# The matrix engine multiplies the former item's values ahead of this item's turns

## The chip, the cores and the metric

One core of one Trainium2 chip runs the whole program. The metric is the device time of one execution in microseconds, median of several runs. The kernel is written in direct instructions for five engines, each with a queue of its own that runs in order: the matrix engine (TensorE, PE), VectorE (DVE), ScalarE (ACT), GpSimd (POOL) and the DMA queues. They wait for one another by semaphores.

## What is computed

512 tokens of width 1024 pass through two layers of a first block (latent attention, "MLA", with 8 heads over all 512 keys, beside a dilated attention with three groups of 8 heads, both gated) and one layer of a second block (a feed-forward part, a linear recurrence beside a windowed attention with 16 heads, a second feed-forward part). All products are made from high and low halves in three matmuls. The parts that the change touches are the three kinds of attention:

```python
# MLA: every query tile of 128 against 512 keys
s = (q_nope @ k_nope + q_rope @ k_rope) * scale
o = softmax(s) @ v
# dilated: three groups, (window, dilation) = (128,1), (512,4), (2048,16)
o_g, lse_g = banded_attention(q_g, k_g, v_g)
out = sum_g softmax(lse)[g] * o_g
# second block: window of 128 keys and a chunk, a bias by distance, a sink logit for each head
p = softmax(concat([q @ k * HEAD_DIM ** -0.5 + bias, sink]))[..., :-1]
o = p @ v
```

## The kernel before

The matrix engine bounds most of the program with long rows of 128x512 matmuls (`feature_major`, `token_major`, the helper `three` in lines 962 to 965). Between them lie seven attentions: `("dil", L, hh)` for two layers and two halves of the heads (8 items each), `("mla", L)` for two layers (16 items each), and `("swa",)` in the second block (16 items). An item is one tile of 128 queries for two heads (four in the second block's, as two pairs), and items run in groups of four tiles, t = 0 to 3. In the second block's attention the item with t = 0 has only half of the keys and is narrower in every step.

For each item n:

- `scores(n)` (PE, line 1085) writes the logits of both halves b = 0, 1 into a pair of PSUM banks; the pairs alternate.
- `maxima(n)` (DVE, line 2049, in MLA line 2060) adds the mask and takes the row maxima.
- `exp_of_item(n)` (ACT, lines 1558, 1562, 1565 and 1572) exponentiates both halves into PR.
- `turn(n)` (PE, line 1097) transposes PR block by block into bank 4 (b = 0) and bank 5 (b = 1). It waits for the exponentials of each half, and for the copy of item n-1 out of the same bank.
- `turned(n)` copies bank 4 (DVE, line 2078) and bank 5 (ACT, line 1583) into PT, which has two buffers.
- `values(n)` (PE, line 1126) waits for both copies and multiplies PT by the values into banks 6 and 7; the last item of a group releases `result`.
- In MLA, at the end of each group, DVE inverts the row sums and spreads them over a tile (`sums_spread`, lines 2086 and 2089), PE transposes them (`spread_sums`, line 1109), and the result is multiplied by them.

DVE and ACT go through the items in the same manner: in round n they first do `maxima(n + 1)` or `exp_of_item(n + 1)` and then `turned(n)`. The first two `scores` of an attention go ahead of the loop, followed by a filler (another product); the loop begins with `turn(n0)`. After the loop come the values of the last item, in MLA with the row sums ahead of them. GpSimd splits two chunks of weights during each attention (`split_in`, lines 892 and 895).

The order of the work is written out by hand: each engine's program is one function, and nothing reorders it.

Of the kernel before, what the change touches and what calls it, by code (L numbers as in the profile page):

```python
# [82 lines left out]
class Plan:  # L83
# [33 lines left out]
    def filler(self, key, by):  # L117

        self.event(key)
        self.pair[key] = 3  # L120
        self.by[key] = by
        out = self.act_out if by == "a" else self.dve_out
        out[key] = len(out) + 1
        self.add_chunk(key, KD, CW, key)
# [220 lines left out]
def build_program(nc, a, out):  # L345
# [3 lines left out]
    with ctx:  # L349
# [155 lines left out]
        def bank(i, n=1):  # L505
            return PS[:, i * S:(i + n) * S]
# [189 lines left out]
        def score_products(it):  # L696

            t, j = it["t"], it["j"]
            tok = slice(t * P, (t + 1) * P)
            got = []  # L700
            if it["kind"] == "mla":
                for i, (q, k) in enumerate(((QNH, KNH), (QNH, KNL), (QNL, KNH))):
                    for b in range(2):
                        got.append((b, 0, S, q[rows_of(b), j, tok], k[rows_of(b), j, :], i == 0))
                for q, k in ((QRH, KRH), (QRH, KRL), (QRL, KRH)):
                    for b in range(2):
                        rows = slice((2 * j + b) % 4 * ROPE, (2 * j + b) % 4 * ROPE + ROPE)
                        got.append((b, 0, S, q[rows, j // 2, tok], k[rows, :], False))
            elif it["kind"] == "dil":
                jj = it["jj"]  # L710
                for block in range(NT):
                    for b in range(2):
                        g = max(block - 1, 0)
                        q, k = (QK[rows_of(b), 2 * g + x, jj, :] for x in range(2))
                        k = near_keys(k, (t - 1 + block) % NT) if block < 2 else k[:, tok]
                        got.append((b, block * P, P, q[:, tok], k, block == 0))
            else:
                n = min(t + 1, 2) * P
                for u in range(2):
                    for b in range(2):  # L720
                        got.append((b, u * 2 * P, n, QS[rows_of(b), 2 * j + u, tok],
                                    K2[rows_of(b), j, (t + 1) * P - n:(t + 1) * P], u == 0))
            return got
# [30 lines left out]
        def blocks_of(it):  # L754
            return (0, 2) if it["kind"] == "swa" and it["t"] == 0 else range(NT)
# [194 lines left out]
        def _(pe):  # L950
            def take_pair(key):

                prev = pl.reuse.get(key)
                if prev is not None:
                    if "x" in pl.by[prev]:
                        pe.wait_ge(f_copied, KD)
                    if "a" in pl.by[prev]:
                        pe.wait_ge(act_out, pl.act_out[prev])
                    if "d" in pl.by[prev]:
                        pe.wait_ge(dve_out, pl.dve_out[prev])  # L960
# [107 lines left out]
            def results_taken(n):  # L1068
                by_dve, by_act = results_before(n)
                if by_dve:  # L1070
                    pe.wait_ge(o_dve, by_dve)
                if by_act:
                    pe.wait_ge(o_act, by_act)

            def attention(name, filler):
                n0, n1 = pl.item_at[name]
                kind = name[0]

                def scores(n):
                    it = pl.items[n]  # L1080
                    take_pair(("item", n))
                    last = [None, None]
                    for b, c0, w, q, k, start in score_products(it):
                        acc = bank(2 * pl.pair["item", n] + b)
                        last[b] = nc.tensor.matmul(acc[:, c0:c0 + w], q, k, start=start, stop=True,  # L1085
                                                   skip_group_check=True)
                    for b in range(2):
                        last[b].then_inc(acc_ready, 1)

                def turn(n):  # L1090
                    it = pl.items[n]
                    for b in range(2):
                        pe.wait_ge(p_ready, 2 * n + 1 + b)
                        if n > 0:
                            pe.wait_ge(pt_act if b else pt_dve, n)
                        for k in blocks_of(it):
                            last = nc.tensor.transpose(bank(4 + b)[:, k * P:(k + 1) * P],  # L1097
                                                       PR[:, n % 2, b * S + k * P:b * S + (k + 1) * P], IDN[:, :])
                        last.then_inc(t_ready, 1)

                def spread_sums(n):

                    it = pl.items[n]
                    g = 4 * it["L"] + it["j"]
                    pe.wait_ge(rl_ready, g + 1)
                    if g:
                        pe.wait_ge(gated_a, g)
                    for t in range(NT):
                        last = nc.tensor.transpose(bank(7)[:, t * P:(t + 1) * P],
                                                   RLB[:, 2 * t:2 * t + 2, :].rearrange("p h d -> p (h d)"), IDN[:, :])  # L1110
                    last.then_inc(rlt_ready, 1)

                def values(n):
                    it = pl.items[n]
                    pe.wait_ge(pt_dve, n + 1)
                    pe.wait_ge(pt_act, n + 1)
                    if it["first"]:
                        results_taken(n)
                    if n == n0:
                        if kind == "swa":  # L1120
                            pe.wait_ge(dve_out, pl.dve_out[filler_of[name]])
                        elif kind == "dil":
                            pe.wait_ge(act_out, pl.act_out[filler_of[name]])
                            pe.wait_ge(v0_in, 16 * 12 * (2 * it["L"] + it["hh"] + 1))
                    for dst, k, v, start, stop in value_products(it):
                        last = nc.tensor.matmul(dst, v, PT[:, n % 2, k * P:(k + 1) * P], start=start, stop=stop,  # L1126
                                                skip_group_check=True)
                    last.then_inc(pv_done, 1)

                scores(n0)  # L1130
                scores(n0 + 1)
                results_taken(n0)
                filler()
                if kind == "mla":
                    pe.wait_ge(act_out, pl.act_out["uv", name[1], 1])
                for n in range(n0, n1):
                    if n0 + 1 < n + 1 < n1:
                        scores(n + 1)
                    turn(n)
                    if n > n0:  # L1140
                        if kind == "mla" and pl.items[n - 1]["last"]:
                            spread_sums(n - 1)
                        values(n - 1)
                if kind == "mla":
                    spread_sums(n1 - 1)
                values(n1 - 1)
# [170 lines left out]
            for L in range(DEPTH):  # L1317
                for hh in range(2):
                    for i, (w, g) in enumerate(DILATED_ORDER):
                        if L == 0 and hh == 0 and i < 2:  # L1320
                            continue
                        if w == "v":
                            if hh == 0 and g == 0:
                                if L == 0:
                                    pe.wait_ge(small_dve, 3)
                                    pe.wait_ge(act_out, pl.act_out["xt", 3])
                                else:
                                    results_taken(pl.item_at["mla", L - 1][1])
                            token_major((w, L, hh, g))
                        else:  # L1330
                            feature_major((w, L, hh, g), new=("x", L) if hh == 0 and i == 0 else None,
                                          norm=("x", L) if hh == 0 and i == 1 else None)
                    pe.wait_ge(rope_done, pl.rope["k", L, hh, 2])
                    attention(("dil", L, hh), lambda: token_major(("v", L, hh, 2)))
# [91 lines left out]
            for j in range(8):  # L1426
                feature_major(("gate", j))
                if j < 4:
# [6 lines left out]
                    for m in range(2):  # L1435
                        for t in range(NT):
                            n = 2 * (NT * m + t)
# [1248 lines left out]
```

## Time and profile before

| | us |
|---|---|
| median of 3 runs | 2161.89 (2161.06 to 2163.26) |
| the profiled execution | 2162.84 |
| its span, first to last instruction | 2161.0 |
| PE busy in it | 2124.9 (98%) |
| DVE, ACT, POOL busy | 1136.9, 765.7, 123.6 |
| PE stalls in front of the turns (line 1097) | 7.5 |
| mean granted clock of PE | 0.997 of 2.4 GHz |

Busy times are of one execution. Starts are in us from the start of the span. A group "x8 1.09" of small matmuls lasts from the first start to the modelled end of the last; the next group on the engine can start before that end, so durations of steps are best taken from start to start.

### The profile page before, as it was taken

How to read it: one execution, taken by the hardware profiler on the slowest of the kernel's cores; microseconds unless marked ns; L12 is line 12 of the kernel's file. 1: busy time of each engine (PE TensorE's matmuls, PEld its weight loads, DVE VectorE, ACT ScalarE, POOL GpSimd, SP SyncE). 2: the span in 40 equal slices, each digit the busy share in tenths (PEclk: the TensorE clock that was granted, in tenths of full speed). 3: DMA queues.
4: the chain of work that ended last, by engine and by line, in shares of the span. 5: the costliest groups of instructions: out<-in, count | busy, mean ns of one | idle time of the engine just before them, and what ended most of it. 6: DMA issues, size and time to landing. Idle time of an engine off the chain costs nothing.

```text
span 2161.0 us, 28431 instructions
## 1 busy us (share of the span) xinstructions
PE 2124.9 (98%) x11767; PEld 1754.6 (81%) x11767; DVE 1136.9 (53%) x1535; ACT 765.7 (35%) x1224; POOL 123.6 (6%) x110
## 2 busy tenths in 40 slices
PE   8999999999999999999999999999999999999998
PEld 6888988678888887788888887787788887888887
DVE  5655557645655557654444445775653446333333
ACT  4251424532242425543222224353643234222222
POOL 0111100200011100200000003000000002000000
PEclk9999999999999999999999999999999999999999
DMA  6313222113313122113333224234022332332321
GB/s 186 99 59 116 80 59 81 40 40 109 100 47 118 60 70 70 40 59 97 97 97 97 98 98 127 79 117 136 21 78 98 98 98 88 96 98 91 100 95 65
DMA packets 158097, 189.04 MB, mean 87 GB/s; under 512 B 4194, under 2 KB 147876, under 8 KB 157860
## 3 DMA queue, kind: packets, MB, share of 16 engines
q1 hardware_dynamic: 153204, 174.41, 25.6%
q0 software_dynamic: 4608, 13.00, 1.9%
q8 instruction: 81, 1.33, 0.3%
q14 instruction: 28, 0.23, 0.0%
q10 hardware_dynamic: 176, 0.07, 0.0%
HBM read 182.20 MB, written 7.36 MB: 88 GB/s over the span
## 4 chain that ended last, share of the span: by engine, by line
PE 91%; DVE 5%; ACT 2%; POOL 1%; issue 1%; DMA 0%; POOLq 0%; DVEq 0%; ACTq 0%
PE PS L963 25%; PE PS L965 25%; PE PS L964 25%; PE PS L1085 5%; PE PS L1126 3%; PE PS L1097 3%; POOL X L930 1%; PE PS L971 1%; PE PS L975 1%; PE PS L972 1%; PE PS L1239 1%; PE PS L1044 0%; DVE WL L1941 0%; DVE UL L1994 0%; DVE TMP L2279 0%
## 5 line engine op out<-in xcount | busy, mean ns | idle before, releaser
L963 PE MATMUL PS<-UH,WH 128*128 128x512 f32 x1632 | 642.7, 394 | 7.5 <-DVE WL L2351 4.7
L965 PE MATMUL PS<-UH,WL 128*128 128x512 f32 x1632 | 637.0, 390 | 0.0
L964 PE MATMUL PS<-UL,WH 128*128 128x512 f32 x1632 | 636.4, 390 | 0.0
L1482 ACT ACTIVATE WH<-WS 128x2048 fp32r<-128x2048 f32 x98 | 187.9, 1918 | 618.1 <-PE PS L965 602.5
L963 PEld LDWEIGHTS PS<-UH,WH 128*128 128x128 f32 x1632 | 307.2, 188 | 75.4 <-DVE UL L1994 6.0
L965 PEld LDWEIGHTS PS<-UH,WL 128*128 128x128 f32 x1632 | 306.9, 188 | 64.7
L964 PEld LDWEIGHTS PS<-UL,WH 128*128 128x128 f32 x1632 | 307.3, 188 | 62.9 <-issue 0.7
L1941 DVE TENSOR_TENSOR WL<-WS,WH 128x2048 fp32r<-128x2048 f32 x98 | 224.4, 2290 | 229.9 <-ACT WH L1482 229.8
L2211 DVE TENSOR_TENSOR WL<-WS,WH 128x2048 fp32r<-128x2048 f32 x44 | 100.7, 2288 | 151.2 <-ACT WH L1636 151.2
L1636 ACT ACTIVATE WH<-WS 128x2048 fp32r<-128x2048 f32 x44 | 84.4, 1917 | 248.9 <-PE PS L965 246.7
L963 PE MATMUL PS<-WH,UH 128*128 128x256 f32 x416 | 118.6, 285 | 0.9 <-DVE PT L2310 0.9
L964 PE MATMUL PS<-WL,UH 128*128 128x256 f32 x416 | 117.7, 283 | 0.0
L965 PE MATMUL PS<-WH,UL 128*128 128x256 f32 x416 | 117.7, 283 | 0.0
L1097 PE MATMUL PS<-IDN,PR 128*128 128x128 f32 x624 | 88.5, 280 | 7.5 <-ACT PT L1583 2.5
L1097 PEld LDWEIGHTS PS<-IDN,PR 128*128 128x128 f32 x624 | 66.7, 140 | 30.8 <-issue 18.2
L1126 PE MATMUL PS<-PT,ARENA 128*64 128x128 f32 x1248 | 84.7, 279 | 0.0
L963 PEld LDWEIGHTS PS<-WH,UH 128*128 128x128 f32 x416 | 79.7, 192 | 2.3 <-issue 1.6
L964 PEld LDWEIGHTS PS<-WL,UH 128*128 128x128 f32 x416 | 79.8, 192 | 0.5 <-issue 0.2
L965 PEld LDWEIGHTS PS<-WH,UL 128*128 128x128 f32 x416 | 79.8, 192 | 0.0
L1126 PEld LDWEIGHTS PS<-PT,ARENA 128*64 128x64 f32 x1248 | 66.6, 136 | 12.6 <-issue 12.6
L2078 DVE COPY PT<-PS 128x512 f32<-128x512 f32 (+1 forms) x80 | 53.8, 672 | 36.1 <-PE PS L1097 36.1
L963 PE MATMUL PS<-HH,WH 128*128 128x512 f32 x176 | 68.5, 389 | 0.0
(312 smaller groups left out, 3090.9 us busy)
## 6 DMA issues: line engine op xcount, KB each, us to landing
WS<-in_ffn_w SPq DMA_DIRECT2D x66, 1024.0 KB, 5.2
WS<-in_w_in SPq DMA_DIRECT2D x61, 1024.0 KB, 5.3
WS<-in_w_out SPq DMA_DIRECT2D x8, 1024.0 KB, 5.1
WS<-in_w_gate SPq DMA_DIRECT2D x8, 1024.0 KB, 5.5
WS<-in_w_attn_out SPq DMA_DIRECT2D x4, 1024.0 KB, 5.1
WS<-in_w_lru_out SPq DMA_DIRECT2D x4, 1024.0 KB, 5.2
WS<-in_w_o SPq DMA_DIRECT2D x4, 1024.0 KB, 5.1
bias_skewed<-bias_rows POOLq DMA_DIRECT2D x1, 3072.0 KB, 13.4
```

Source lines behind the costliest of these rows:

```text
L930: nc.gpsimd.tensor_tensor(X[:, k, :], old[:, k, :], SUMMED[k][:, :], ALU.add).then_inc(x_new, 1)
L963: nc.tensor.matmul(dst, sh, mh, start=start, stop=False, skip_group_check=True)
L964: nc.tensor.matmul(dst, sh, ml, start=False, stop=False, skip_group_check=True)
L965: return nc.tensor.matmul(dst, sl, mh, start=False, stop=stop, skip_group_check=True)
L1085: last[b] = nc.tensor.matmul(acc[:, c0:c0 + w], q, k, start=start, stop=True, skip_group_check=True)
L1097: last = nc.tensor.transpose(bank(4 + b)[:, k * P:(k + 1) * P], PR[:, n % 2, b * S + k * P:b * S + (k + 1) * P], IDN[:, :])
L1126: last = nc.tensor.matmul(dst, v, PT[:, n % 2, k * P:(k + 1) * P], start=start, stop=stop, skip_group_check=True)
L1482: nc.scalar.activation(WH[:, c % 2, 0:kt * n], staged(c, kt * n), ACT.Copy).then_inc(w_hi, 1)
L1636: nc.scalar.activation(WH[:, c % 2, :], WS[:, c % 2, :], ACT.Copy).then_inc(w_hi, 1)
L1941: tt(WL[:, c % 2, 0:kt * n], staged(c, kt * n), WH[:, c % 2, 0:kt * n].bitcast(F32), ALU.subtract).then_inc(w_split, 1)
L2078: nc.vector.tensor_copy(used_half(it, PT[:, n % 2, 0:S]), used_half(it, bank(4))).then_inc(pt_dve, 1)
L2211: tt(WL[:, c % 2, :], WS[:, c % 2, :], WH[:, c % 2, :].bitcast(F32), ALU.subtract).then_inc(w_split, 1)
```

## The change

In the loop of `attention` in the matrix engine's program, `values(n - 1)`, and in MLA at group ends `spread_sums(n - 1)` with it, go ahead of `turn(n)`. Before, round n issued scores(n+1), turn(n), values(n-1); after, it issues scores(n+1), values(n-1), turn(n). All seven attentions use this loop. The programs of the other engines, all waits and all buffers stay as they are.

```diff
                 for n in range(n0, n1):
                     if n0 + 1 < n + 1 < n1:
                         scores(n + 1)
-                    turn(n)
                     if n > n0:
                         if kind == "mla" and pl.items[n - 1]["last"]:
                             spread_sums(n - 1)
                         values(n - 1)
+                    turn(n)
                 if kind == "mla":
                     spread_sums(n1 - 1)
                 values(n1 - 1)
```

## Rows read from the trace of the kernel before

**Rows 1.** The page, busy us by engine, share of the span and instructions.

```profile
PE 2124.9 (98%) x11767; PEld 1754.6 (81%) x11767; DVE 1136.9 (53%) x1535; ACT 765.7 (35%) x1224; POOL 123.6 (6%) x110
```

**Rows 2.** Groups by line: busy us, mean ns, idle before and its releasers.

```profile
L1097 PE MATMUL PS<-IDN,PR 128*128 128x128 f32 x624 | 88.5, 280 | 7.5 <-ACT PT L1583 2.5 <-ACT ARENA L1790 2.2 <-DVE PT L2078 1.8
```

**Rows 3.** Windows, first to last attention: busy of PE, PEld, DVE, ACT, POOL; PEclk; DMA.

```profile
125.40:1557.40 1432.00, 1416.66 (x8429) 1164.97 (x8427) 817.02 (x1230) 540.80 (x978) 99.94 (x76) 1.00 0.26 82
```

**Rows 4.** Timeline, first dilated attention, steady state: start, us, engine, line, operation.

```profile
129.54 1.16 PE L1085 MATMUL PS<-ARENA 64*128 64x128 f32 x16
130.63 1.09 PE L1097 MATMUL PS<-IDN,PR 128*128 128x128 f32 x8
131.66 1.09 PE L1126 MATMUL PS<-PT,ARENA 128*64 128x128 f32 x16
132.68 1.16 PE L1085 MATMUL PS<-ARENA 64*128 64x128 f32 x16
133.45 0.61 ACT L1583 ACTIVATE PT<-PS 128x512 f32<-128x512 f32 x1
133.77 1.09 PE L1097 MATMUL PS<-IDN,PR 128*128 128x128 f32 x8
```

**Rows 5.** Timeline, tail of the same attention (its last item is number 7).

```profile
142.10 1.16 PE L1085 MATMUL PS<-ARENA 64*128 64x128 f32 x16
...
145.62 0.63 PE L1097 MATMUL PS<-IDN,PR 128*128 128x128 f32 x4 [0.31 <-DVE PT L2078]
146.01 0.61 ACT L1583 ACTIVATE PT<-PS 128x512 f32<-128x512 f32 x1
146.76 0.63 PE L1097 MATMUL PS<-IDN,PR 128*128 128x128 f32 x4 [0.51 <-ACT PT L1583]
147.32 1.97 PE L1126 MATMUL PS<-PT,ARENA 128*64 128x128 f32 x32
147.43 0.60 ACT L1583 ACTIVATE PT<-PS 128x512 f32<-128x512 f32 x1 [0.81 <-PE PS L1097]
```

**Rows 6.** Timeline, head of the same attention: scores(2) and ScalarE's copy of item 0.

```profile
126.40 1.16 PE L1085 MATMUL PS<-ARENA 64*128 64x128 f32 x16
127.08 0.62 ACT L1583 ACTIVATE PT<-PS 128x512 f32<-128x512 f32 x1
```

**Rows 7.** Timeline, tail of the first MLA attention (its last item is number 15).

```profile
441.94 0.51 PE L1085 MATMUL PS<-KNH,QNH 64*128 64x512 f32 x2
...
443.73 1.09 PE L1097 MATMUL PS<-IDN,PR 128*128 128x128 f32 x8
445.87 1.40 PE L1097 MATMUL PS<-IDN,PR 128*128 128x128 f32 x8
445.91 0.59 ACT L1583 ACTIVATE PT<-PS 128x512 f32<-128x512 f32 x1
447.37 0.43 DVE L2089 COPY ARENA<-RLM 128x512 f32<-128x512 f32 x1
448.23 0.66 PE L1109 MATMUL PS<-IDN,ARENA 128*128 128x128 f32 x4
```

**Rows 8.** Timeline, first MLA attention, end of its first group.

```profile
402.31 2.11 DVE L2089 COPY ARENA<-RLM 128x512 f32<-128x512 f32 x1
404.02 1.09 PE L1097 MATMUL PS<-IDN,PR 128*128 128x128 f32 x8
```

**Rows 9.** Timeline, second block's attention: scores of items 11 and 15, copies, narrow values.

```profile
1538.27 1.14 PE L1085 MATMUL PS<-ARENA 64*128 64x256 f32 x8
...
1548.54 0.39 ACT L1583 ACTIVATE PT<-PS 128x256 f32<-128x256 f32 x1
1549.64 0.66 PE L1126 MATMUL PS<-PT,ARENA 128*64 128x128 f32 x8
1550.22 1.14 PE L1085 MATMUL PS<-ARENA 64*128 64x256 f32 x8
...
1554.19 0.61 ACT L1583 ACTIVATE PT<-PS 128x512 f32<-128x512 f32 x1
```

## The prediction

> **What bounds the kernel now.** I read first the busy shares. The matrix engine is busy for 2124.9 of 2161.0 us [rows 1], so a delay on it is a delay of the end, and a gain can only come out of the 36 us in which it stood. Next the groups by line, for its stalls at the transposes, the "turn": 7.5 us over 624 instructions, mostly released by the two copies into PT [rows 2]. This is all that the profile has to offer to work that fills the wait in front of a turn. Then the timeline of the steady state of an attention, where the order of the work decides [rows 4].
>
> I write S(n), T(n), V(n) for the scores, the turn and the values of item n. S writes one bank pair, VectorE takes the maxima, ScalarE exponentiates both halves, T turns them into banks 4 and 5, VectorE copies bank 4 and ScalarE bank 5 into PT, V multiplies PT. ScalarE does the exponentials of item n+1 *before* its copy of item n. So the copy of item n comes late, however early T(n) was.
>
> In the dilated attention [rows 4]: S(n+1) starts at 129.54, T(n) at 130.63, V(n-1) at 131.66, S(n+2) at 132.68. That is S 1.09, T 1.03, V 1.02, 3.14 us an item with no gap. The ScalarE copy of item n starts at 133.45 and ends at 134.06, 4.52 us after S(n+1) started. Before, the first to wait for it is the second half of T(n+1), at 133.77 + 0.51 = 134.28. The copy is ready 0.22 us ahead of it, and hidden.
>
> **The change, part by part.** It adds and removes no instruction and no DMA. The matmuls of V(n-1), its waits for both copies of item n-1, and at group ends of the MLA attention the four transposes of the row sums with their waits, go ahead of T(n). ScalarE, VectorE and GpSimd keep their orders. Behind the waiting V stand, on the matrix engine's queue, T(n) and S(n+2), and behind these all three other engines' work for the next items.
>
> *Constants.* From the end of a copy to the matrix engine's start: 146.01 + 0.61 = 146.62 to 146.76, 0.14 us. A half turn that starts after a wait takes 0.56 (146.76 to 147.32) for half of 1.03, so 0.05 for starting again. From the start of a half turn to its copy 0.67 (146.76 to 147.43) [rows 5]. No row shows V itself waiting. Its release and restart could cost nothing, if its weights are loaded while it waits, or the whole gap of 0.31 us that a half turn shows behind a copy [rows 5]. I take 0.14 and 0.05, because V waits for the same two semaphores on the same engine as the half turn.
>
> *The dilated loop.* Now V(n) stands right behind S(n+2). It could start when S(n+2) is through, at 133.77 by the old clock, but the copy of item n allows 134.06 + 0.14 = 134.20: the 0.22 us of cover have become 0.43 us of lateness. The chain is S(n+1), 4.52 to the end of the copy, 0.14, V(n) 0.05 + 1.02, T(n+1) 1.03, and then S(n+3): 6.76 us for two items, where the matrix engine's own work is 6.28. The turn in this order starts a V later, but its second half plus 0.67 still comes before the exponentials of the next item end, so it isn't what the copy waits for. VectorE's copy is earlier still.
> At the head, S(2) starts at 126.40 and the ScalarE copy of item 0 ends at 127.70, since the results of the filler lie ahead of it [rows 6]. V(0) starts at 127.84, so S(3) comes 1.44 + 0.05 + 2.05 = 3.54 us behind S(2). From S(3) to S(5) to S(7) are two rounds of 6.76: S(7) is 17.06 us behind S(2), before it was 142.10 - 126.40 = 15.70. Loss 1.36 us.
>
> *The dilated tail.* Before, S(7) at 142.10, then the last values end at 147.32 + 1.97 = 149.29, 7.19 us later. The two halves of T(7) wait there (145.62 and 146.76), but V(6) and V(7) run in one piece of 32, since V(6) covers the copy of item 7 [rows 5]. After: V(6) at 4.66 behind S(7), T(7) at 5.73, its second half at 6.24, copy from 6.91 to 7.52, and V(7), with nothing left to cover the copy, from 7.66, to 1.09 + 0.05 later: 8.80. Loss 1.61 us. One dilated attention loses 2.97; the trace has four of the same shape: **11.9 us**.
>
> *The MLA loop.* S takes 1.79 us (441.94 to 443.73), and the copy ends at 445.91 + 0.59 = 446.50, 4.56 behind S. V(n) comes up only at 1.79 + 2.05 + 1.79 = 5.63. Cover 0.93 us, no loss, no gain. At the tail V(14) starts at 4.70, T(15) at 5.77; from its start the row sums are spread by VectorE in 447.80 - 445.87 = 1.93, so they arrive at 7.84, and spread (0.58), restart and V(15) end at 9.49, where it was 448.23 + 0.58 + 1.02 = 449.83, 7.89 [rows 7]. Loss 1.60. In the first group of each layer the copy of the row sums takes 2.11 us and ends at 404.42, while a later one takes 0.43 [rows 7, 8]. The matrix engine is through with S(5) at 404.02 and now wants these sums at once: 404.42 + 0.14 - 404.02 + 0.05 = 0.59, which T(4) used to cover. (Bounds: 0, if the later turn lets that copy run at 0.43, and 1.) The MLA layers lose 2.2 each, **4.4 us**.
>
> *The second block's attention.* With all items full the ScalarE copy ends 1554.19 + 0.61 - 1550.22 = 4.58 behind S. A round of two full items is 4.58 + 0.14 + 0.05 + 2.05 = 6.82. Where item n is a first of its group, its copy takes 0.39 instead of 0.61 and its V 0.58: 4.36 + 0.14 + 0.05 + 0.58 + 1.03 = 6.16. Four items make 12.98, where the trace has 1550.22 - 1538.27 = 11.95 [rows 9]. From item 3 to 15 that is three times 1.03, 3.1 us; the tail has the shapes of the dilated one, 1.6. Together **4.7 us**.
>
> *Sum.* 11.9 + 4.4 + 4.7 = **21.0 us** lost. The profiled execution took 2162.84 us (span 2161.0), the median is 2161.89. So 2183.8 for a profile, and about 2183 for the median. I find nothing that gives it back: the stages behind an attention are matrix engine work without gaps, and their weights arrive no later.
>
> **The rivals.**
> *Tails alone.* If something in the loop shortens ScalarE's chain by 0.43 us (exponentials that start earlier than the old order shows), the rounds stay at 6.28 and only the tails and sums remain: 4 x 1.61 + 4.4 + 1.6 = 12.4, so 2174. Against it: the chain begins at S and holds nothing that the change touches.
> *No recovery.* In my rounds a late V is followed by one that is nearly on time. If each V were late by 0.43 + 0.05, a dilated attention loses 7 x 0.48 + 1.61 = 5.0, the second block's 15 x 0.5 + 1.6 = 9.1, MLA 4.4: 33, so 2195. It needs a copy that starts after the turn and not after the exponentials; turn to copy to V is 0.51 + 0.67 + 0.61 + 0.14 + 1.07 = 3.00 an item, just under 3.14.
> *Faster.* The values fill the wait of the turn. The turn's stalls of 7.5 us in [rows 2], and the two waits of each tail, would shrink, by some 9 us at most: 2153. (A dilated tail of 7.19 us holds 1.09 + 1.03 + 1.02 + 1.03 + 2.04 + 0.06 = 6.27 of work, so 0.9 in each of seven tails, and the rest in the second block's loop.) This happens if the copy into PT ends before S(n+2) does. It decides at 0.43 us: MLA's long S meets it, the two others miss it in [rows 4, 9].
> *No effect.* The lateness in the loop is balanced by stalls that vanish, 2162 within 4 us: the same two facts at half size.
> *The clock.* The granted clock is 1.00, the 2.4 GHz level, from the first attention to the last [rows 3], through gaps of 0.5 us. Should more gaps take it to 1.2 GHz in the dilated attentions and the second block's, their 4 x 22.9 + 4 x 11.95 = 139 us would double: 2301. The Trainium skill has such a case (TensorE: Matmul & The Clock Gate, "A second HAM failure mode: psum-queue depth-cycling"): frequent short idle times between groups of matmuls made the clock swing between its levels. By that rule, with the same gaps at other places, this kernel should have swung already; the trace doesn't agree.
>
> **How the numbers follow.** Forecast 0.71 (its own range 2178 to 2189: the wait of V from 0 to 0.1 above my constants over some 45 waits, the MLA bound), tails alone 0.10, no recovery 0.05, faster 0.06, no effect 0.06, the clock 0.02. The range 2173 to 2190 holds the first two. 0.2%, about 4.3 us, is what a measurement can tell. Faster 0.06, same 0.06, slower 0.88.
>
> **What would show it.** In the profile after: L1126 gets stalls released by ACT PT L1583, about 0.4 us each, most of all at every second item of the dilated attentions, and L1097 loses its own. S(3) to S(5) in the first dilated attention is 6.76 us, S(7) to the first matmul behind it 8.7. The MLA period stays 3.84 between group ends. Four items of the second block's attention take 13.0. If the dilated round is still 6.28, the step of the copy's lateness is wrong; if it is near 7.2, the recovery is. If PEclk leaves 1.00, all of it is.

## The result and the profile after

The changed kernel takes 2184.9 us in the median of 4 runs (2183.4 to 2185.7), the kernel before 2161.5 (2161.1 to 2163.3). The ratio is 1.0107, 95% interval 1.0095 to 1.0119. The prediction said 2183 and 21.0 us lost; 23.4 were. The profiled execution took 2185.72 us, its span is 2183.9, 22.9 us longer than the span before.

The page first: busy shares, the chain that ended last by engine, and two groups of section 5.

```profile
PE 2126.5 (97%) x11767; PEld 1756.4 (80%) x11767; DVE 1143.1 (52%) x1535; ACT 767.9 (35%) x1224; POOL 123.6 (6%) x110
...
PE 88%; DVE 5%; ACT 4%; issue 2%; POOL 1%; DMA 0%; POOLq 0%; DVEq 0%; ACTq 0%
...
L1126 PE MATMUL PS<-PT,ARENA 128*64 128x128 f32 x1248 | 85.8, 278 | 24.8 <-ACT PT L1583 17.2
...
L1097 PE MATMUL PS<-IDN,PR 128*128 128x128 f32 x624 | 85.4, 279 | 2.2 <-ACT ARENA L1790 2.2
```

The matrix engine does the same work (2126.5 us against 2124.9 in [rows 1]) and stands longer. The stalls have changed places: the turn's 7.5 us of [rows 2] fell to 2.2, and the 2.2 are the wait of the two first MLA turns that was there before. The values never stood before the change and now stand for 24.8. Their row in the view of groups by line of the kernel before:

```profile
L1126 PE MATMUL PS<-PT,ARENA 128*64 128x128 f32 x1248 | 84.7, 279 | 0.0
```

The turn's waits behind the two copies did vanish, as the change intends, and the values' waits cost more than four times as much.

What the values wait for is in the view of the waits on the matrix engine (us in total, times, longest):

```profile
PE PS L1126 <- ACT PT L1583: 17.2, 24, 1.5
PE PS L1126 <- ACT ARENA L1590: 6.4, 7, 1.2
...
PE PS L1109 <- DVE ARENA L2089: 2.6, 4, 0.9
```

The first row is ScalarE's copy of bank 5 into PT, the last one shown the spread row sums of MLA. Both were in the prediction. The second wasn't: ScalarE's copy of a finished group's *results* out of bank 7. Seven times is four dilated attentions with one inner group start, and the second block's with three.

The timeline of the first dilated attention (start, us, engine, line), matrix engine and, where they release it, ScalarE's copies:

```profile
126.97 1.16 PE L1085 MATMUL PS<-ARENA 64*128 64x128 f32 x16
128.37 1.09 PE L1126 MATMUL PS<-PT,ARENA 128*64 128x128 f32 x16 [0.23 <-ACT PT L1583]
...
130.41 1.16 PE L1085 MATMUL PS<-ARENA 64*128 64x128 f32 x16
...
135.07 1.09 PE L1126 MATMUL PS<-PT,ARENA 128*64 128x128 f32 x16 [0.23 <-ACT PT L1583]
136.10 1.09 PE L1097 MATMUL PS<-IDN,PR 128*128 128x128 f32 x8
137.12 1.16 PE L1085 MATMUL PS<-ARENA 64*128 64x128 f32 x16
...
141.03 0.60 ACT L1583 ACTIVATE PT<-PS 128x512 f32<-128x512 f32 x1
141.51 0.62 ACT L1590 ACTIVATE ARENA<-PS 128x512 f32<-128x512 f32 x1
142.27 1.09 PE L1126 MATMUL PS<-PT,ARENA 128*64 128x128 f32 x16 [0.71 <-ACT ARENA L1590]
...
144.32 1.16 PE L1085 MATMUL PS<-ARENA 64*128 64x128 f32 x16
...
148.98 1.09 PE L1126 MATMUL PS<-PT,ARENA 128*64 128x128 f32 x16 [1.45 <-ACT PT L1583]
150.00 1.10 PE L1097 MATMUL PS<-IDN,PR 128*128 128x128 f32 x8
151.88 1.09 PE L1126 MATMUL PS<-PT,ARENA 128*64 128x128 f32 x16 [0.78 <-ACT PT L1583]
```

From S(3) at 130.41 to S(5) at 137.12 is a round of 6.71 us; the prediction had 6.76. From there to S(7) at 144.32 are 7.20. In that round V(4) belongs to a new group, and it starts 0.14 us after the result copy ended at 142.13; the copy into PT had ended at 141.63. At the tail V(6) starts 4.66 us behind S(7), to the hundredth as predicted, and the attention ends at 152.97, 8.65 behind S(7), where [rows 5] have 7.19.

First turn and last values of the first MLA attention and of the second block's, in the kernel before:

```profile
389.67 1.09 PE L1097 MATMUL PS<-IDN,PR 128*128 128x128 f32 x8 [1.11 <-ACT ARENA L1790]
...
448.81 1.09 PE L1126 MATMUL PS<-PT,ARENA 128*64 128x128 f32 x16
...
1510.82 0.60 PE L1097 MATMUL PS<-IDN,PR 128*128 128x128 f32 x4
...
1555.50 1.97 PE L1126 MATMUL PS<-PT,ARENA 128*64 128x128 f32 x32
```

and in the changed one, with the scores of items 11 and 15 of the second block's attention:

```profile
396.47 1.09 PE L1097 MATMUL PS<-IDN,PR 128*128 128x128 f32 x8 [1.11 <-ACT ARENA L1790]
...
458.37 1.09 PE L1126 MATMUL PS<-PT,ARENA 128*64 128x128 f32 x16
...
1528.04 0.60 PE L1097 MATMUL PS<-IDN,PR 128*128 128x128 f32 x4
...
1558.27 1.14 PE L1085 MATMUL PS<-ARENA 64*128 64x256 f32 x8
...
1571.64 1.13 PE L1085 MATMUL PS<-ARENA 64*128 64x256 f32 x8
...
1579.25 1.09 PE L1126 MATMUL PS<-PT,ARENA 128*64 128x128 f32 x16 [0.78 <-ACT PT L1583]
```

| from these rows, us | before | after | lost | predicted |
|---|---|---|---|---|
| dilated, S(2) to the end (of four) | 22.89 | 26.00 | 3.11 | 2.97 |
| MLA, first turn to the end (of two) | 60.23 | 62.99 | 2.76 | 2.2 |
| second block's, the same | 46.65 | 52.30 | 5.65 | 4.7 |

4 x 3.11 + 2 x 2.76 + 5.65 = 23.6 us, beside 22.9 between the spans. The seven attentions hold the whole loss; where the 0.7 went is told below, behind the rivals.

### The profile page after: what moved, and what is told of

It reads as the page before. It is cut to its first block, busy times and chain, and to the rows that moved or that the text cites. A ratio compares the mean times of both kernels' runs of the same rounds, so it can differ in the third digit from the quotient of the medians.

```text
span 2183.9 us, 28431 instructions
## 1 busy us (share of the span) xinstructions
PE 2126.5 (97%) x11767; PEld 1756.4 (80%) x11767; DVE 1143.1 (52%) x1535; ACT 767.9 (35%) x1224; POOL 123.6 (6%) x110
## 4 chain that ended last, share of the span: by engine, by line
PE 88%; DVE 5%; ACT 4%; issue 2%; POOL 1%; DMA 0%; POOLq 0%; DVEq 0%; ACTq 0%
PE PS L963 25%; PE PS L965 25%; PE PS L964 25%; PE PS L1085 4%; PE PS L1126 3%; PE PS L1097 2%; POOL X L930 1%; PE PS L971 1%; PE PS L975 1%; PE PS L972 1%; ACT PT L1583 1%; PE PS L1239 1%; ACT PR L1565 1%; PE PS L1044 0%; ACT ARENA L1519 0%
## 5 line engine op out<-in xcount | busy, mean ns | idle before, releaser
L1126 PE MATMUL PS<-PT,ARENA 128*64 128x128 f32 x1248 | 85.8, 278 | 24.8 <-ACT PT L1583 17.2
```

## The experiments

The theory: the values wait for ScalarE's copy, and that is late because it stands behind the exponentials of the next item. The main rival: it is late because the turn itself now stands behind the values. Besides, whether each attention loses by itself, and what the missing term is. Each run was timed in five or more rounds beside the kernel before, which took 2161.4 us in the first set of four and 2161.5 in the second.

**The dilated attentions alone.**

```diff
+                    if not (kind == "dil"):
+                        turn(n)
                     if n > n0:
                         ...
                         values(n - 1)
-                    turn(n)
+                    if kind == "dil":
+                        turn(n)
```

> The new order in the four dilated attentions alone; MLA and the second block's attention keep the old one. Theory (the values wait for ScalarE's late copy, and each attention loses by itself): each dilated attention takes 27.0 us from its first turn to its last values as in the changed kernel (23.9 before), 3.1 us more, four of them 12.4 us, so about 2174, and the other three attentions keep their old lengths (60.2, 60.2, 46.7). Rival (the loss comes from later stages that the shifted work disturbs): the four attentions explain less than the whole loss of this kernel, or the stages between them change length.

Measured: 2173.5 us, ratio 1.0052 (1.0038 to 1.0066), 12.1 us more than before. Its first dilated attention has scores at 129.68, 136.39 and 143.59, rounds of 6.71 and 7.20 again. In the trace each of the four takes 26.98 us from its first turn to its last values, as expected, and the others keep 60.24 (MLA) and 46.67 (the second block's). The loss is where the order is changed, and adds up without the others.

**MLA alone**, the same with `kind == "mla"`.

> The new order in the two MLA attentions alone. Theory: no stall in the loop but at group ends, where the transposes of the row sums and the first values of the next group wait (0.4 and 0.15 us), and the tail loses 1.44: each MLA attention takes 2.76 us more than its 60.2, together 5.5, about 2167. The dilated attentions keep 23.9 and the second block's 46.7. Rival (MLA loses nothing by itself, its scores being long enough to cover every copy): 2161.5.

Measured: 2166.1 us, ratio 1.0023 (1.0014 to 1.0033), 4.6 us more. The first MLA attention takes from 388.11 to 451.11, 63.0 us, and the second the same: 5.5 us more in both, where the medians show 4.6 (why they can differ is told below, behind the rivals). The second block's attention keeps 46.69. So MLA pays though its loop is covered; its price is at the group ends and the tail.

**The last round in the old order**, in all seven (`if n < n1 - 1` in place of `kind == "dil"`).

> The changed kernel, but the last round of each attention issues the turn ahead of the former item's values, as before. Theory: the loops keep their loss, the tails get back 1.46 us (dilated, four), 1.44 (MLA, two) and 1.45 (second block), 10.2 us together: about 2174.7; from the last scores of a dilated attention to the end of its last values 7.2 us again and not 8.65. Rival (a tail is only slow because the loop ahead of it brought ScalarE late): the tail stays between 7.9 and 8.65 and the kernel above 2179.

Measured: 2174.9 us, ratio 1.006 (1.0046 to 1.0074). The tail after S(7) at 143.61 (lines behind the edit stand 3 lower: L2081 is VectorE's copy, L1586 ScalarE's):

```profile
147.26 0.63 PE L1097 MATMUL PS<-IDN,PR 128*128 128x128 f32 x4 [0.44 <-DVE PT L2081]
148.28 0.63 PE L1097 MATMUL PS<-IDN,PR 128*128 128x128 f32 x4 [0.39 <-ACT PT L1586]
148.84 1.97 PE L1126 MATMUL PS<-PT,ARENA 128*64 128x128 f32 x32
```

It ends at 150.81, 7.20 behind S(7), as before. With the turn in front, V(6) again runs while item 7 is copied, and the loop ahead leaves nothing behind in the tail. 10 of the 23.4 us are the seven last rounds.

**ScalarE's copy ahead of the exponentials.**

```diff
                 for n in range(n0, n1):
-                    if n0 + 1 < n + 1 < n1:
-                        exp_of_item(n + 1)
-                    turned(n)
                     if n > n0 and pl.items[n - 1]["last"] and not mla:
                         result(pl.items[n - 1])
+                    turned(n)
+                    if n0 + 1 < n + 1 < n1:
+                        exp_of_item(n + 1)
```

> The changed kernel, but in each round ScalarE copies item n out of bank 5 (and the finished group's results ahead of that) before it takes the exponentials of item n+1; before it did so after them. Theory (the values wait because ScalarE's copy stands behind the exponentials): the stalls in the loops go, a dilated item takes 3.14 to 3.25 us instead of 3.36, four items of the second block's attention 12.0 to 12.4 instead of 13.37, the stall at the first values of a group goes, the tails lose about 1.2 us instead of 1.45: about 2174, between 2171 and 2178. Rival (the turn now stands behind the values, so its copies and the next values come a turn later whatever ScalarE's order): no better than 2184, and worse if the exponentials come late.

Measured: 2174.2 us, ratio 1.0052 (1.0039 to 1.0066), 10.7 less than the changed kernel. One item of its loop:

```profile
133.09 1.16 PE L1085 MATMUL PS<-ARENA 64*128 64x128 f32 x16
133.20 0.60 ACT L1583 ACTIVATE PT<-PS 128x512 f32<-128x512 f32 x1 [0.75 <-PE PS L1097]
133.69 0.47 ACT L1562 ACTIVATE PR<-PS,NAT 128x256 f32<-128x256 f32 x1
...
134.19 1.09 PE L1126 MATMUL PS<-PT,ARENA 128*64 128x128 f32 x16
135.21 1.11 PE L1097 MATMUL PS<-IDN,PR 128*128 128x128 f32 x8
136.25 1.16 PE L1085 MATMUL PS<-ARENA 64*128 64x128 f32 x16
```

The copy ends at 133.80 and the values start at 134.19, right behind the scores, without a wait. An item takes 3.16 us. The turn still stands behind the values, as in the changed kernel. So the rival falls: ScalarE's order made the loop's stalls. The tails keep most of theirs (S(7) at 142.66, end 150.92: 8.26), since there no scores are left to cover a copy. From first turn to last values a dilated attention now takes 25.40 us (26.97 in the changed kernel, 23.85 before), the second block's 47.77 (52.30, 46.65), and MLA, whose loss lies elsewhere, 62.94 (63.0, 60.24). This order is still 12.8 us behind the kernel before.

**ScalarE's copy ahead of the exponentials, in the kernel before** (the matrix engine's old order; the result copy stays behind the exponentials).

> The kernel before (turn ahead of the former item's values), but ScalarE copies item n out of bank 5 ahead of the exponentials of item n+1. Theory (two chains compete: scores, maxima, exponentials, copy; and turn, copy, exponentials, next turn): the second becomes the bound here, 0.67 from half turn to copy, 0.61, 1.81 of exponentials, 0.14, 0.05: 3.28 us for a dilated item where the matrix engine has 3.14 of work, and about 12.5 for four items of the second block's attention instead of 11.95; MLA stays at 3.84. Some 3 us more in the dilated attentions, 1.5 in the second block's: about 2166. Rival (the copy ahead of the exponentials is better whatever the matrix engine's order): 2158 to 2162.

Measured: 2165.2 us, ratio 1.0014 (1.0005 to 1.0023), 3.7 more than before. The direction was as expected, the sizes in the trace were smaller: an item takes 3.16 us where 3.28 were expected, and four items of the second block's attention 12.12 where 12.5 were. The rows above show the missed part: the next activation starts 0.49 us after the copy's start (133.20 to 133.69), not after its 0.60. In the trace the seven attentions lose 2.2 us together; the rest of the 3.7 is within what the short stretches of lower clock described below make of a median. With either order of the matrix engine ScalarE's copy ahead of the exponentials stays behind the kernel before.

**Without the result copies inside an attention.** This kernel leaves part of the computation out: ScalarE's half of the results of all groups but the last is not kept.

```diff
-                if it["kind"] != "mla":
+                if it["kind"] != "mla" and it is items[-1]:
                     self.o_act += 1
...
-                dst = OUN[:, it["j"], 1, :] if it["kind"] == "dil" else OSU[:, 2 * it["j"] + 1, :]
-                nc.scalar.activation(dst, bank(7), ACT.Copy).then_inc(o_act, 1)
+                for j in ((it["j"] - 1, it["j"]) if it["kind"] == "dil" else range(4)):
+                    dst = OUN[:, j, 1, :] if it["kind"] == "dil" else OSU[:, 2 * j + 1, :]
+                    ins = nc.scalar.activation(dst, bank(7), ACT.Copy)
+                ins.then_inc(o_act, 1)
...
                     turned(n)
-                    if n > n0 and pl.items[n - 1]["last"] and not mla:
-                        result(pl.items[n - 1])
```

> The changed kernel without ScalarE's copy of bank 7 at the end of each group inside an attention (the results of those groups are left out; the last group's bank is copied into their places after the loop), so the first values of a group wait for nothing of ScalarE but the copy into PT. Theory (the term missing from the prediction is this copy, 0.5 us behind the other): the dilated round with a group start goes from 7.20 back to 6.71 us (0.49 each in four attentions), four items of the second block's attention from 13.37 to about 12.97 (0.4 each, three times): 3.2 us less than the changed kernel, about 2181.7. Rival (the wait is for the copy into PT and the other is only the last to be named): rounds of 7.20 and 13.37 stay, 2184.9.

Measured: 2181.3 us, ratio 1.0089 (1.0075 to 1.0103), 3.6 less than the changed kernel. The round with the group start:

```profile
136.89 1.16 PE L1085 MATMUL PS<-ARENA 64*128 64x128 f32 x16
...
141.50 1.09 PE L1126 MATMUL PS<-PT,ARENA 128*64 128x128 f32 x16 [0.18 <-ACT PT L1583]
142.53 1.09 PE L1097 MATMUL PS<-IDN,PR 128*128 128x128 f32 x8
143.55 1.16 PE L1085 MATMUL PS<-ARENA 64*128 64x128 f32 x16
```

6.66 us instead of 7.20, and four items of the second block's attention (S(11) at 1556.01, S(15) at 1568.84) 12.83 instead of 13.37: 0.54 each, seven times, 3.8 us, and by the same 3.8 the attentions are shorter from first turn to last values (26.42 for 26.97, 50.70 for 52.30). The missing term is this copy.

**Both copies into PT on VectorE**, in the dilated and the second block's attention, with the new order.

```diff
-                    turned(n)
+                    if mla:
+                        turned(n)
...
+                if it["kind"] != "mla":
+                    dve.wait_ge(t_ready, 2 * n + 2)
+                    nc.vector.tensor_copy(used_half(it, PT[:, n % 2, S:]), used_half(it, bank(5))).then_inc(pt_act, 1)
```

> The changed kernel, but in the dilated and the second block's attention VectorE copies both banks into PT and ScalarE none. Theory (it is when the copies into PT end that sets the values, not which engine or how much work it has): VectorE's second copy ends 4.17 us behind the scores, so the values start at 4.31 instead of 4.66 and a round of two dilated items is about 6.4 us, not 6.71; the first values of a group now wait for VectorE's result copy, at about 5.0, and that round stays near 7.1. Four items of the second block's attention about 12.5 instead of 13.37; the tails stay. 5 us less than the changed kernel, about 2179.5. Rival (ScalarE's exponentials are late themselves and hold the turn): rounds of 6.71 and 13.37 stay.

Measured: 2179.8 us, ratio 1.0085 (1.0071 to 1.0099), 5.1 less than the changed kernel. Scores at 129.61, 135.92 and 142.93: rounds of 6.31 and 7.01. Four items of the second block's attention take 12.64. The exponentials keep ScalarE as long as before, and the stalls that are left follow the copies to the other engine (12.1 us of waits for VectorE's copies into PT, in place of 17.2 for ScalarE's): it is the time at which the copy ends that counts. The round of 7.01 holds the wait for VectorE's copy of a finished group's results, 0.65 us, as expected.

**A version for the old order**: VectorE makes both copies into PT (the same edit), ScalarE both copies of a group's results; VectorE's own copy of bank 6 is taken out, which the diff here doesn't show.

```diff
-                dst = OUN[:, it["j"], 1, :] if it["kind"] == "dil" else OSU[:, 2 * it["j"] + 1, :]
-                nc.scalar.activation(dst, bank(7), ACT.Copy).then_inc(o_act, 1)
+                for i, done in enumerate((o_dve, o_act)):
+                    dst = OUN[:, it["j"], i, :] if it["kind"] == "dil" else OSU[:, 2 * it["j"] + i, :]
+                    nc.scalar.activation(dst, bank(6 + i), ACT.Copy).then_inc(done, 1)
```

> The kernel before with its old order of the matrix engine, but in the dilated and the second block's attention VectorE makes both copies into PT and ScalarE both copies of a group's results. Meant to beat both. Theory (what is left to gain in the old order is the wait of the last turn and the second block's stalls, both behind ScalarE's copy): in a dilated tail the second half of the last turn starts about 4.2 us behind the last scores instead of 4.66, 0.4 us each in four tails; four items of the second block's attention fall from 11.95 to about 11.6, three times; about 3 us less than before, 2158.5. Rival (VectorE with both copies is full, 3.0 of 2.9 us for an item of the second block's attention, and late with the maxima): that attention gets longer than 46.7 us and the time is 2162 or more.

Measured: 2158.1 us, ratio 0.9985 (0.9976 to 0.9994): 3.3 us less than the kernel before and 27 less than the changed one (each against its own runs of the kernel before, 2161.5 in both). Its last dilated round (L2080 and L2083 are VectorE's copies of banks 4 and 5):

```profile
145.37 0.68 DVE L2083 COPY PT<-PS 128x512 f32<-128x512 f32 x1
...
145.59 1.23 PE L1097 MATMUL PS<-IDN,PR 128*128 128x128 f32 x8 [0.31 <-DVE PT L2080]
...
146.75 2.04 PE L1126 MATMUL PS<-PT,ARENA 128*64 128x128 f32 x32
```

S(7) stood at 142.07, so the end comes 6.72 behind it and not 7.19. In the second block's attention four items take 11.60 (S(11) at 1534.20, S(15) at 1545.80), where [rows 9] have 11.95. The attentions together are 3.2 us shorter in the trace, beside the 3.3 in the medians. What could be had out of the stalls of [rows 2] lay in the time of the copies, not in this order of the matrix engine.

## Why the prediction was right, step by step

- *What bounds.* Right. All of the loss lies in the seven attentions, and nothing gave it back.
- *The dilated loop.* Right: 6.71 us for 6.76. Of the constants the 0.14 held (142.13 to 142.27), and the 0.05 for starting again did not: the turn follows the late values by 1.03 (135.07 to 136.10), as without a wait. A late V is followed by one that is nearly on time (waits of 1.39 - 1.09 = 0.30 and 0.14 in turn). That settles "no recovery".
- *The step that failed* is the list of the waits of V as those "for both copies of item n-1": it left out the third, that the first values of a group wait until the last group's results are out of banks 6 and 7. The code says so (`results_taken`), and the experiment without this copy measures it: 0.54 us in each of seven rounds (7.20 for 6.66, and 13.37 for 12.83), 3.8 us, and 3.6 in the medians. In the old order the turn hid this wait; the row of the values there has 0.0 idle. In MLA the result is VectorE's, and behind each of three inner group starts the values come 0.15 later than elsewhere (scores to values 1.94 us for 1.79), 0.9 in both layers. That this is the same wait is read from the code; the trace names none there, and no run took it away.
- *The tails.* Right in kind, 0.15 too large each: 1.46, 1.44 and 1.45 for 1.61, 1.60 and 1.6, for the same 0.05 that was counted for each wait. 1.0 us in seven tails.
- *The MLA sums.* Predicted 0.59 for the first group of each layer; the scores to the transposes of the sums took 2.28 us (409.00 to 411.28) where 1.79 is the rule, so 0.49. The copy of the sums took 1.71 us there, not 2.11, since it started later and ended with the same GpSimd instruction. The measured value lies between the bounds named.
- *The MLA group ends* hold a second small loss that the prediction put at nothing: 0.14 us at each of three, 0.8 in both layers. Over the second group end it is 4.42 us from scores to scores (425.57 to 429.99), and was 4.29 (418.02 to 422.31). The four transposes of the row sums followed the turn after 0.93 and had the values 0.53 behind them; now the turn takes its full 1.02 and the transposes 0.58. Why, no run shows.
- *The rounds and heads.* The dilated head took 3.44 for 3.54 us, the first round 6.71 for 6.76, the second without the result copy 6.66, and four items of the second block's attention without it 12.83 for 12.98. These terms were 0.25 too large in each dilated attention and 0.45 in the second block's, 1.5 us in all.
- Together: 21.0 + 3.8 + 0.9 + 0.8 - 1.0 - 0.2 - 1.5 = 23.8, for 23.6 in the table. That 21.0 came so near is in part luck: 5.5 us of waits were left out and 2.7 counted too much. The mechanism of the larger part, the late copy into PT in loops and tails, doesn't rest on that.
- *The rivals.* "Tails alone" falls by the round of 6.71, "faster" and "no effect" by the 24.8 us in front of the values. These two had a point that came true: the turn's own stalls behind the copies did vanish. As to the clock: in each of the seven attentions it is 1.00, its 2.4 GHz level, through 36 waits of up to 1.5 us in front of values and row sums. From the first attention to the last the view gives

```profile
125.40:1580.40 1455.00, 1418.80 (x8434) 1167.31 (x8433) 823.24 (x1231) 543.04 (x979) 99.91 (x76) 1.00 0.26 81
```

By the case in the Trainium skill (TensorE: Matmul & The Clock Gate, "A second HAM failure mode: psum-queue depth-cycling") such idle times between groups can make the clock swing. In these attentions they did not.

But the 1.00 of this row, and that of [rows 3], is a rounded mean, and the prediction read too much into it. Two stretches of 3.4 us at 0.50, the 1.2 GHz level, lie inside each: from 355.5 and from 1348.8 us in the changed kernel, from 348.0 and from 822.4 in the kernel before. All four are between attentions. Just before the one at 355.5 the matrix engine had been busy for 3.06 of 3.40 us (352.1 to 355.5), and in it it was busy all the time. What one costs shows in the stage from a layer's second dilated attention to its MLA in the changed kernel: 113.6 us in the first layer, which has it (282.87 to 396.47), 112.0 in the second, which has none (765.77 to 877.75). So 1.6 us, and as much for each of the two in the kernel before. The one at 1348.8 cost 0.3: its stage took 450.4 us for 450.1 in the kernel before, which has none there.

That explains two differences. The attentions lose 23.6 us and the spans differ by 22.9: the kernel before paid 3.2 us for its two stretches and the changed one 1.9, and 0.6 us were lost ahead of the first attention, which wasn't followed further. And the times of the kernel before beside the second set of experiments come in three groups, 2159.7 to 2160.1, 2161.0 to 2162.1 and 2162.7 to 2163.3, steps of the same 1.6 us, so a median can move by one step without any change in an attention. The lowest run with MLA alone is 5.3 us above the lowest of these, beside the 5.5 of its trace. With 12.5 for the dilated attentions alone that leaves 5.6 for the second block's, as in the table, though it was not run alone.

## What to carry to other kernels

Moving work ahead to fill a wait moves its own waits ahead too: before the move, look up how long every one of them has been satisfied, including those that the old order never had to name. Here the copy into PT had 0.22 us of cover in the loop and the move took 0.65 away. And when two steps of a pipeline alternate on one engine, look at the order of the engine that serves both: here changing ScalarE's order too gave back 10.7 of the 23.4 us, and in the old order the same edit cost some. Neither beat the old pair; what did was another engine that brings the late copy sooner.

## What was not expected of the hardware

- A ScalarE copy with a row of 0.60 us keeps ScalarE from its next activation for only 0.49 (133.20 to 133.69; 0.48 from 141.03 to 141.51). In such a chain through one engine, count from start to start, and take the whole row only for the last member.
- VectorE's spreading copy takes 0.43 us [rows 7], and 2.11 or 1.71 where a GpSimd instruction runs beside it, and in both kernels it ended 0.3 us after that instruction. In the changed kernel that instruction and the copy are

```profile
404.38 1.89 POOL L892 CAST WH<-WS 128x2048 fp32r<-128x2048 f32 x1
406.36 4.58 POOL L895 TENSOR_TENSOR WL<-WS,WH 128x2048 fp32r<-128x2048 f32 x1
...
409.51 1.71 DVE L2089 COPY ARENA<-RLM 128x512 f32<-128x512 f32 x1
```

  with ends at 410.94 and 411.22. In the kernel before they are at 404.13 and 404.42. The copy started 1.82 us ahead of the instruction's end there and 1.43 ahead of it here, and ended no sooner for the earlier start.
- A wait in front of values cost its length and nothing for starting again (the turn follows at 1.03, waited or not), and so did the one in front of the first MLA turn (396.47 to the scores at 397.49, 1.02). Why the half turn of [rows 5] takes 0.56 and not 0.51, no run shows.
- The clock dropped to its 1.2 GHz level for 3.4 us, twice, in the middle of a program whose matrix engine is busy for 97% of it, and a rounded mean of 1.00 over 1400 us hides that.
